# Feed-forward output of a two-layer decoder step: four of eight output tiles computed as two pairs of seven products for the last six inner tiles

## The chip, the cores and the metric

The kernel runs on one core of a Trainium2 chip. The metric is the device time of one execution, in microseconds. The engines are TensorE (PE, with its weight loads PEld), VectorE (DVE), ScalarE (ACT), GpSimd (POOL) and SyncE (SP), which here issues the loads from HBM.

## What is computed

One inference step of two layers for 512 prompt tokens and 64 sample tokens (576 columns, handled as two halves of 288). Each layer has a feed-forward block ahead of its mixer and one behind it, so there are four feed-forward passes. The change is in the output product of each pass, `(silu(a) * b) @ w_out`:

```
D_MODEL = 1024
D_FF = 2816
...
def half_swiglu(x, g, w_in, w_out):
    a, b = jnp.split(rms_norm(x, g) @ w_in, 2, axis=-1)
    return x + 0.5 * ((jax.nn.silu(a) * b) @ w_out)
...
for i in range(DEPTH):
    x = half_swiglu(x, norm_w[i, 0], w_ffn_in[i, 0], w_ffn_out[i, 0])
    x = x + mixer_i(rms_norm(x, norm_w[i, 1]))
    x = half_swiglu(x, norm_w[i, 2], w_ffn_in[i, 1], w_ffn_out[i, 1])
```

## The kernel before

**Numbers.** Every factor is split into a high part (`hw`, `hh`, `uah`) and a low part (`lw`, `hl`, `ual`); a product of 128 x 128 weights with 288 columns is made three times: high by high, high by low, low by high. Activations lie with features on partitions: D_MODEL is 8 tiles of 128 (`x[:, m, :]`), D_FF is 22 inner tiles (`TILES`).

**Units.** A pass is `NU = 30` units. Units 0 and 1 compute inner tiles in the plain way, the other inner tiles and most of the output by the scheme of Strassen in Winograd's form: blocks 1 to 7 ("products", `times(s, p)`) in place of eight. Four of the seven need differences of weight blocks (`diff1`, `diff2`, `diff34` on VectorE into `tw`, their high parts by `high12` and `high34` on ScalarE, their low parts by `low12` and `low34` on VectorE), three take the blocks as they come (`direct`: a copy and a negation on ScalarE, then an accumulating transfer issued by GpSimd, `add_direct`). On the other side they need sums and differences of halves of the hidden tiles (`h_side3`, `h_sides` on VectorE, places S1 to S4 of `hr`; high parts by `high_hs`, low parts by `low_hs`).

**Where the output is made.** Inner tiles 0 to 7 and 8 to 15 go into the output by the units 9 to 12 and 21 to 24 (`FAST_OUT`), each a pair of output tiles, 4 x 3 matrix products in each of the seven; VectorE adds each product to `x` (`add_product`), and the next product into the same bank waits for that (`x_part`). The last `KO = 6` inner tiles, 16 to 21, are multiplied plainly after the last unit: eight output tiles of 6 x 3 x 2 = 36 matrix products. `first_outs` interleaves tiles 0 and 1 with product 4 of the last unit; `out` does the others, which wait for `x_done`, the addition of the tile two before; the last tile of the last pass is made by halves. ScalarE makes the high part of each tile's weights (`high_out`, L1056), GpSimd the low part by a subtraction (L828), SyncE loads them (`out_unit`, L619). VectorE adds a whole tile to `x` (`add_out`, L2620) and right after that prepares tile m for what follows: the low part for the mixer (`low_u`, L2288) or, after the second pass, the sides of the next pass (`side` L2365, `side_sums` L2372 to L2378, `low_s` L2352), and adds squares for the norm (L2294).

**What sets the order.** Each engine's program is written out by hand, and semaphores with counts connect them: `prod_done` counts products of TensorE, `x_part` and `x_done` additions, `unit_done` output tiles. An instruction waits with everything behind it on its engine. Nothing is scheduled by a planner; `product_order` and `update_order` only number the products and additions.

**The last unit before the end**, `inner` of unit 29: VectorE does `gate_half` (L2399) of the tile before, its `hidden` (L2407), its low part (L2420), and then five operations of `sums` (L2428 to L2439), with `add_product` at L2476 in output units.

## Time and profile before

| what | us |
|---|---|
| median of 3 runs | 2453.65 (2452.84 to 2457.1) |
| profiled execution, whole | 2449.32 |
| its span in the trace | 2447.5 |
| first end: from the first output tile of the first pass to the mixer's first product | 350.04 to 390.1 |
| second end (followed at once by the third pass) | 1281.2 to 1321.3 |
| third end | 1656.8 to 1696.9 |
| fourth end, up to the tile by halves | 2393.8 to 2434.0 |

In the profile's views a line such as L2620 is a line of the kernel; "sb_" stands ahead of tiles in on-chip memory, "ps" is the accumulator memory of TensorE. Idle time is put down to the wait that ended last. The profiled execution is one run, and 4.3 us below the median of the others.

### The profile page before, as it was taken

The page shows a single profiled execution, that of the slowest core. Times are in us where ns is not written, and L with a number is a line of the kernel's source. Part 1 is how long each engine was busy: PE and PEld are TensorE (multiplying, and loading weights), DVE is VectorE, ACT ScalarE, POOL GpSimd, SP SyncE. Part 2 cuts the span into 40 slices and gives each one's busy share as a digit, 9 for nine tenths or more (in the row PEclk, how much of TensorE's full clock was granted, in tenths as well). Part 3 has the DMA queues.
Part 4 walks back from the last instruction along what each step waited for, and adds up shares of the span by engine and source line. Part 5 has one row for each costly group of instructions (what it writes and reads, how often), then busy time and mean ns, then how long its engine had stood idle before and what let it go on. Part 6 is the DMA issues. An engine that isn't in the chain of part 4 may idle for free.

```text
span 2447.5 us, 50261 instructions
## 1 busy us (share of the span) xinstructions
PE 2414.4 (99%) x19713; PEld 2362.0 (97%) x19713; DVE 1837.7 (75%) x3054; ACT 1392.9 (57%) x2388; POOL 755.4 (31%) x739
## 2 busy tenths in 40 slices
PE   8999999999999999999999999999999999999998
PEld 8999999999999989999999999999999998999998
DVE  8979766977777788978876988875235438988875
ACT  7757553545555556757666766664223227767663
POOL 1222224545555542222223222224322321222222
PEclk9999999999999999999999999999999999999999
DMA  6677753133333325676765677764433434677762
GB/s 192 162 170 166 171 118 111 49 103 106 106 106 97 106 83 147 152 177 160 175 139 137 150 172 162 172 148 134 158 131 122 136 110 111 158 172 162 174 149 88
DMA packets 105686, 339.01 MB, mean 139 GB/s; under 512 B 13776, under 2 KB 17360, under 8 KB 87184
## 3 DMA queue, kind: packets, MB, share of 16 engines
q1 hardware_dynamic: 53936, 242.40, 30.0%
q0 software_dynamic: 51552, 93.87, 22.8%
q8 instruction: 137, 2.24, 0.4%
q14 instruction: 61, 0.50, 0.1%
HBM read 223.06 MB, written 19.32 MB: 99 GB/s over the span
## 4 chain that ended last, share of the span: by engine, by line
PE 94%; DVE 4%; ACT 1%; issue 1%; DMA 0%; SPq 0%; POOL 0%; DVEq 0%; ACTq 0%
PE ps L1644 17%; PE ps L1642 17%; PE ps L1652 17%; PE ps L1540 7%; PE ps L1548 7%; PE ps L1541 7%; PE ps L1661 2%; PE ps L1662 2%; PE ps L1669 2%; PE ps L1591 1%; PE ps L1581 1%; PE ps L1582 1%; PE ps L1980 1%; PE ps L1982 1%; PE ps L1981 1%; DVE sb_acc L2713 1%
## 5 line engine op out<-in xcount | busy, mean ns | idle before, releaser
L1644 PE MATMUL ps<-sb_ual,sb_hw 128*128 128x288 f32 x2240 | 614.2, 296 | 0.0
L1642 PE MATMUL ps<-sb_uah,sb_hw 128*128 128x288 f32 x2240 | 610.7, 295 | 0.1
L813 POOL DMA_DIRECT2D sb_lw<-sb_rawf x328 | 282.3, 866 | 961.6 <-ACT sb_lw L987 944.8
L1642 PEld LDWEIGHTS ps<-sb_uah,sb_hw 128*128 128x128 f32 x2240 | 421.0, 188 | 0.7 <-issue 0.5
L1644 PEld LDWEIGHTS ps<-sb_ual,sb_hw 128*128 128x128 f32 x2240 | 421.2, 188 | 0.0
L796 POOL TENSOR_TENSOR sb_wl<-sb_raw,sb_wh 128x512 fp32r<-128x512 f32 (+1 forms) x170 | 282.4, 1678 | 389.8 <-ACT sb_wh L956 377.3
L1652 PE MATMUL ps<-sb_uah,sb_lw 128*128 128x288 f32 x2240 | 385.0, 294 | 0.0
L1540 PE MATMUL ps<-sb_uh,sb_wh 128*128 128x288 f32 x1360 | 373.6, 301 | 0.1
L1541 PE MATMUL ps<-sb_ul,sb_wh 128*128 128x288 f32 x1360 | 366.8, 296 | 0.0
L1652 PEld LDWEIGHTS ps<-sb_uah,sb_lw 128*128 128x128 f32 x2240 | 328.3, 188 | 0.7 <-DVE sb_lw L2336 0.4
L1540 PEld LDWEIGHTS ps<-sb_uh,sb_wh 128*128 128x128 f32 x1360 | 255.7, 188 | 7.6 <-issue 5.0
L985 ACT CAST sb_hw<-sb_rawf 128x512 fp32r<-128x512 f32 x336 | 207.7, 618 | 87.8 <-PE ps L1652 72.6
L1541 PEld LDWEIGHTS ps<-sb_ul,sb_wh 128*128 128x128 f32 x1360 | 255.8, 188 | 0.5
L1644 PE MATMUL ps<-sb_hl,sb_hw 128*128 128x288 f32 x896 | 243.9, 295 | 0.0
L1642 PE MATMUL ps<-sb_hh,sb_hw 128*128 128x288 f32 x896 | 243.2, 293 | 0.0
L956 ACT CAST sb_wh<-sb_raw 128x1024 fp32r<-128x1024 f32 (+1 forms) x106 | 111.5, 1052 | 199.6 <-PE ps L1548 127.5
L2341 DVE TENSOR_TENSOR sb_lw<-sb_tw,sb_hw 128x1024 fp32r<-128x1024 f32 x112 | 137.1, 1224 | 92.7 <-ACT sb_hw L1022 88.6
L987 ACT ACTIVATE sb_lw<-sb_rawf 128x512 fp32r<-128x512 f32 x328 | 206.5, 629 | 0.0
L1548 PE MATMUL ps<-sb_uh,sb_wl 128*128 128x288 f32 x1360 | 195.3, 296 | 0.2 <-POOL sb_wl L796 0.2
L1022 ACT CAST sb_hw<-sb_tw 128x1024 fp32r<-128x1024 f32 x112 | 117.7, 1051 | 124.2 <-PE ps L1652 124.2
L1548 PEld LDWEIGHTS ps<-sb_uh,sb_wl 128*128 128x128 f32 x1360 | 186.1, 190 | 0.9 <-POOL sb_wl L796 0.5
L1644 PEld LDWEIGHTS ps<-sb_hl,sb_hw 128*128 128x128 f32 x896 | 168.4, 188 | 0.0
(366 smaller groups left out, 5096.3 us busy)
## 6 DMA issues: line engine op xcount, KB each, us to landing
sb_lw<-sb_rawf POOLq DMA_DIRECT2D x358, 256.0 KB, 3.7
sb_rawf<-w_ffn_in SPq DMA_DIRECT2D x87, 1024.0 KB, 5.0
sb_rawf<-w_ffn_so SPq DMA_DIRECT2D x32, 1024.0 KB, 5.0
sb_raw<-w_ssd SPq DMA_DIRECT2D x64, 512.0 KB, 3.6
sb_raw<-w_att SPq DMA_DIRECT2D x40, 512.0 KB, 3.7
sb_rawf<-w_ffn_out SPq DMA_DIRECT2D x32, 384.0 KB, 3.1
sb_h<-state SPq DMA_DIRECT2D x8, 1024.0 KB, 5.1
ssm_sample<-sb_h SPq DMA_DIRECT2D x8, 1024.0 KB, 4.8
```

Of the source, the lines that this page charges most:

```text
L796: ins = pool.tensor_tensor(wl[parity][:, c], raw[:, parity, c], wh[parity][:, c].bitcast(F32), ALU.subtract)
L813: pool.dma_start(slot(lw, p), rawf[:, s % 2, i * BL:(i + 1) * BL], accum_op=ALU.add).then_inc(ld_in[i], 16)
L985: nc.scalar.copy(slot(hw, p), src).then_inc(hd_done, 1)
L987: nc.scalar.activation(slot(lw, p), src, ACT.Copy, scale=-1.0).then_inc(nd_done, 1)
L1022: nc.scalar.copy(slot(hw, 7, 2), tw[:, 2 * BL:4 * BL]).then_inc(ht34_done, 1)
L1540: pe.matmul(ps[:, b, 0:n], w, rh[:, k, t0:t0 + n], start=first and k == 0, stop=False)
L1541: pe.matmul(ps[:, b, 0:n], w, rl[:, k, t0:t0 + n], start=False, stop=False)
L1548: ins = pe.matmul(ps[:, b, 0:n], w, rh[:, k, t0:t0 + n], start=False, stop=last and k == nk - 1)
L1642: pe.matmul(out, w[:, k * P:(k + 1) * P], high[k], start=begins and k == 0, stop=False, skip_group_check=True)
L1644: pe.matmul(out, w[:, k * P:(k + 1) * P], low[k], start=False, stop=False, skip_group_check=True)
L1652: ins = pe.matmul(out, v[:, k * P:(k + 1) * P], high[k], start=False, stop=k == 3, skip_group_check=True)
L2341: V.tensor_tensor(slot(lw, 7, 2), tw[:, 2 * BL:4 * BL], slot(hw, 7, 2).bitcast(F32), ALU.subtract).then_inc(lt34_done, 1)
```

## The change

A pass has two more units, 30 and 31 (`NU = 32`, `E0`, `E1`). They make output tiles 2, 3 and 4, 5 from inner tiles 16 to 21 as seven products of 3 x 3 matrix products each. Output tiles 0, 1 and 6, 7 (`OUT_TILES`) stay plain, 36 matrix products each. So:

- The last six inner tiles form three pairs (`c == 2`); `h_side3`, `h_sides`, `high_hs` and `low_hs` now run for them too. Their fourth sum (A12 less S2) has a place of its own, `hr[:, 3, ...]`, with its own high part (`high_s4_out`) and low part (`low_s4_out`). Tiles 20 and 21 are kept in `he` and `ge`.
- SyncE loads tiles 0 and 1, then the two new units (`w_ffn_se`, 4 x 384 columns), then tiles 6 and 7. ScalarE and GpSimd get three `direct` blocks for each new unit, and four tiles instead of eight. The weight places of the new units are in another order (`END_SLOT`).
- On VectorE the last `gate_half` stands ahead of the first difference of weights of unit 30, as does the rest of the tile's end; then come the additions of the new units, mixed with the preparation of finished tiles (`next_sides`), in the order 0, 1, 3, 2, 5, 4, 6, 7 (`ORDER`), which the readers of the prepared tiles follow.
- On TensorE the units stand between `first_outs` and tile 6; product 4 of unit 31 stands within tile 6.

```diff
-NU = 30
+NU = 32
+OUT_TILES = (0, 1, 6, 7)
+END_SLOT = {1: 3, 5: 4, 6: 5, 2: 6, 3: 0, 7: 1, 4: 2}
...
                 first_outs(f)
-                for m in range(2, KD - 1 if f == 3 else KD):
-                    out(f, m)
+                s = f * NU + E0
+                for p in (1, 2, 5, 6, 3, 7):
+                    times(s, p)
+                times(s + 1, 1)
+                times(s + 1, 5)
+                times(s, 4)
+                times(s + 1, 6)
+                times(s + 1, 2)
+                times(s + 1, 3)
+                times(s + 1, 7)
+                u = U_FFN[f] + OUT_TILES.index(6)
+                free_out(f, 6)
+                pe.wait_ge(wh_done, u + 1)
+                out_highs(f, 6, range(2))
+                times(s + 1, 4)
+                out_highs(f, 6, range(2, KO))
+                pe.wait_ge(wl_done, u + 1)
+                out_lows(f, 6, range(KO)).then_inc(unit_done, 1)
+                if f < 3:
+                    out(f, 7)
...
                 gate_half(last)
+                diff1(e)
                 hidden(last)
+                diff2(e)
                 low_h(last)
+                diff34(e)
+                h_sides(f, 2, 2)
+                low12(e)
+                low_hs(f, 2, 2)
+                low_s4_out(f)
+                diff1(e1)
+                diff2(e1)
...
+                add_product(e, 1)
+                add_out(0)
+                add_out(1)
+                add_product(e, 2)
+                add_product(e, 5)
+                low34(e)
+                add_product(e, 6)
+                diff34(e1)
+                low12(e1)
+                add_product(e, 3)
+                add_product(e, 7)
+                next_sides(0)
+                add_product(e1, 1)
+                add_product(e1, 5)
+                next_sides(1)
+                add_product(e, 4)
+                add_product(e1, 6)
+                low34(e1)
+                add_product(e1, 2)
+                add_product(e1, 3)
+                add_product(e1, 7)
+                next_sides(3)
+                add_product(e1, 4)
+                next_sides(2)
+                next_sides(5)
+                next_sides(4)
+                add_out(6)
...
                 last = f * NU + LAST
+                direct(last + 1, 1)
                 silu(last)
                 high_h(last)
+                high12(last + 1)
+                direct(last + 1, 2)
+                high_hs(f, 2, 2)
+                direct(last + 1, 3)
+                high_s4_out(f)
+                high34(last + 1)
```

The first place is VectorE around the end of unit 29 in the first pass. Before, `sb_hr` and `sb_hl` are the tile of unit 28 (hidden and its low part), then come the five sums, the last gate, and the last tile:

```order
L2407 TENSOR_TENSOR sb_hr<-sb_hr,sb_gr 128x2x288
L2420 TENSOR_TENSOR sb_hl<-sb_hr,sb_hh 128x2x288
L2428 TENSOR_TENSOR sb_gr<-ps,sb_gr 128x288
L2431 TENSOR_TENSOR sb_hr<-ps,sb_hr 128x288
L2435 TENSOR_TENSOR sb_gr<-sb_gr,sb_rms 128x288
L2437 TENSOR_TENSOR sb_hr<-sb_hr,sb_pc 128x288
L2439 TENSOR_TENSOR sb_hr<-sb_hr,sb_rms 128x576
L2399 TENSOR_TENSOR sb_gr<-ps,sb_rms 128x288
L2407 TENSOR_TENSOR sb_hr<-sb_hr,sb_gr 128x576
L2420 TENSOR_TENSOR sb_hl<-sb_hr,sb_hh 128x576
L2620 SCALAR_TENSOR_TENSOR sb_x<-ps,sb_x 128x576
```

Now, at the same place (`sb_he` is tile 20):

```order
L2500 TENSOR_TENSOR sb_he<-sb_he,sb_gr 128x576
L2540 TENSOR_TENSOR sb_hr<-sb_he 128x288
L2514 TENSOR_TENSOR sb_hl<-sb_he,sb_hh 128x2x288
L2562 TENSOR_TENSOR sb_hl<-sb_hr,sb_hh 128x864
L2522 TENSOR_TENSOR sb_gr<-ps,sb_gr 128x288
L2525 TENSOR_TENSOR sb_ge<-ps,sb_ge 128x288
L2529 TENSOR_TENSOR sb_gr<-sb_gr,sb_rms 128x288
L2531 TENSOR_TENSOR sb_ge<-sb_ge,sb_pc 128x288
L2533 TENSOR_TENSOR sb_ge<-sb_ge,sb_rms 128x576
L2492 TENSOR_TENSOR sb_gr<-ps,sb_rms 128x288
```

Two operations (L2540, L2562) have come in between the hidden tile and the five sums. Between that last gate (L2492) and the first addition to x (L2585) now stand:

```order
L2410 TENSOR_TENSOR sb_tw<-sb_rawf 128x512
L2500 TENSOR_TENSOR sb_ge<-sb_ge,sb_gr 128x576
L2416 TENSOR_TENSOR sb_tw<-sb_rawf,sb_tw 128x512
L2514 TENSOR_TENSOR sb_hl<-sb_ge,sb_hh 128x576
L2423 TENSOR_TENSOR sb_tw<-sb_rawf,sb_tw 128x1024
L2549 TENSOR_TENSOR sb_hr<-sb_ge,sb_he 128x288
L2550 TENSOR_TENSOR sb_hr<-sb_ge,sb_hr 128x288
L2552 TENSOR_TENSOR sb_hr<-sb_ge,sb_hr 128x288
L2429 TENSOR_TENSOR sb_lw<-sb_tw,sb_hw 128x1024
L2562 TENSOR_TENSOR sb_hl<-sb_hr,sb_hh 128x864
L2568 TENSOR_TENSOR sb_hl<-sb_hr,sb_hh 128x864
L2410 TENSOR_TENSOR sb_tw<-sb_rawf 128x512
```

(and one more L2416). Before, two of these twelve stood there. The second place is ScalarE at the same time. Before, after the copy of the last sum (L1032), `silu`, the high part of the tile and the weights of output tiles:

```order
L1032 COPY sb_hr<-ps 128x288
L1037 ACTIVATE sb_gr<-sb_gr 128x576
L1043 CAST sb_hh<-sb_hr 128x576
L1056 CAST sb_hw<-sb_rawf 128x768 x2
L967 ACTIVATE sb_uh<-sb_x,sb_gains 128x576
```

Now:

```order
L1070 COPY sb_ge<-ps 128x288
L1021 CAST sb_hw<-sb_rawf 128x512
L1023 ACTIVATE sb_lw<-sb_rawf 128x512
L1075 ACTIVATE sb_gr<-sb_gr 128x576
L1081 CAST sb_hh<-sb_ge 128x576
L1050 CAST sb_hw<-sb_tw 128x1024
L1021 CAST sb_hw<-sb_rawf 128x512
L1023 ACTIVATE sb_lw<-sb_rawf 128x512
L1086 CAST sb_hh<-sb_hr 128x864
L1021 CAST sb_hw<-sb_rawf 128x512
L1023 ACTIVATE sb_lw<-sb_rawf 128x512
L1090 CAST sb_hh<-sb_hr 128x864
```

The blocks of the new unit stand between the steps of the last tile, and the high part of the fourth sums (L1090) stands behind two of them. The third place is VectorE in the second end, ahead of the additions of output tiles 6 and 7 (L2740). Before, the addition of tile 6 (L2620) stood behind the preparation of tile 5:

```order
L2620 SCALAR_TENSOR_TENSOR sb_x<-ps,sb_x 128x576
L2365 SCALAR_TENSOR_TENSOR sb_ual<-sb_x,sb_gains,sb_uah 128x2x288
L2372 SCALAR_TENSOR_TENSOR sb_us<-sb_x,sb_gains,sb_us 128x288
L2375 TENSOR_TENSOR sb_us<-sb_us 128x288
L2377 TENSOR_TENSOR sb_us<-sb_us 128x288
L2378 SCALAR_TENSOR_TENSOR sb_s<-sb_x,sb_gains,sb_us 128x288
L2294 TENSOR_TENSOR sb_ssq<-sb_ssq,sb_sqx 128x576
L2352 TENSOR_TENSOR sb_ual<-sb_us,sb_uah 128x3x288
L2620 SCALAR_TENSOR_TENSOR sb_x<-ps,sb_x 128x576 x2
```

Now the preparation of tiles 5 and 4 stands in one piece behind the last product's addition and that of tile 2:

```order
L2458 SCALAR_TENSOR_TENSOR sb_ual<-sb_x,sb_gains,sb_uah 128x2x288
L2383 TENSOR_TENSOR sb_ssq<-sb_ssq,sb_sqx 128x576
L2458 SCALAR_TENSOR_TENSOR sb_ual<-sb_x,sb_gains,sb_uah 128x2x288
L2465 SCALAR_TENSOR_TENSOR sb_us<-sb_x,sb_gains,sb_us 128x288
L2468 TENSOR_TENSOR sb_us<-sb_us 128x288
L2470 TENSOR_TENSOR sb_us<-sb_us 128x288
L2471 SCALAR_TENSOR_TENSOR sb_s<-sb_x,sb_gains,sb_us 128x288
L2383 TENSOR_TENSOR sb_ssq<-sb_ssq,sb_sqx 128x576
L2445 TENSOR_TENSOR sb_ual<-sb_us,sb_uah 128x3x288
L2740 SCALAR_TENSOR_TENSOR sb_x<-ps,sb_x 128x576 x2
```

The same group of L2458 to L2445 stands twice more ahead of it, for tiles 0 and 1 and for tiles 3 and 2.

## Rows read from the trace of the kernel before

**Rows 1.** The page: busy time by engine, and the last chain by engine.
```profile
PE 2414.4 (99%) x19713; PEld 2362.0 (97%) x19713; DVE 1837.7 (75%) x3054; ACT 1392.9 (57%) x2388; POOL 755.4 (31%) x739
...
PE 94%; DVE 4%; ACT 1%; issue 1%; DMA 0%; SPq 0%; POOL 0%; DVEq 0%; ACTq 0%
```

**Rows 2.** Windows over first and second end: length, busy by engine, clock, DMA.
```profile
350.04:390.10 40.06, 40.00 (x303) 39.77 (x302) 23.46 (x28) 16.36 (x24) 14.13 (x8) 1.00 0.27 83
1281.20:1321.30 40.10, 40.04 (x302) 39.65 (x301) 27.73 (x41) 21.61 (x35) 13.80 (x8) 1.00 0.35 112
```

**Rows 3.** Chain in order of time, first end: start us, us, what.
```profile
364.96 1.57 PE ps L1669 x12
...
369.72 1.57 PE ps L1669 x12
```

**Rows 4.** Line L2620 (output tile added to x): who waited for it, us, times.
```profile
  PEld ps L1661: 1.3, 5
```

**Rows 5.** VectorE's timeline, first end: start us, us, instruction, idle before it.
```profile
347.99 1.73 DVE L2420 TENSOR_TENSOR sb_hl<-sb_hr,sb_hh 128x576 fp32r<-128x576 f32 x1 [0.74 <-ACT sb_hh L1043]
349.64 0.45 DVE L2428 TENSOR_TENSOR sb_gr<-ps,sb_gr 128x288 f32<-128x288 f32 x1
...
350.37 1.37 DVE L2435 TENSOR_TENSOR sb_gr<-sb_gr,sb_rms 128x288 f32<-128x288 f32 x1
...
352.14 0.76 DVE L2439 TENSOR_TENSOR sb_hr<-sb_hr,sb_rms 128x576 f32<-128x576 f32 x1
353.06 0.46 DVE L2399 TENSOR_TENSOR sb_gr<-ps,sb_rms 128x288 f32<-128x288 f32 x1 [0.16 <-PE ps L1652]
354.27 0.76 DVE L2407 TENSOR_TENSOR sb_hr<-sb_hr,sb_gr 128x576 f32<-128x576 f32 x1 [0.75 <-ACT sb_gr L1037]
355.77 0.76 DVE L2420 TENSOR_TENSOR sb_hl<-sb_hr,sb_hh 128x576 fp32r<-128x576 f32 x1 [0.74 <-ACT sb_hh L1043]
```

**Rows 6.** GpSimd's timeline, first end.
```profile
347.26 4.16 POOL L828 TENSOR_TENSOR sb_lw<-sb_rawf,sb_hw 128x768 fp32r<-128x768 f32 x2 [6.50 <-ACT sb_hw L1056]
```

**Rows 7.** Groups of VectorE, whole span: busy us, mean ns, idle before.
```profile
L2341 DVE TENSOR_TENSOR sb_lw<-sb_tw,sb_hw 128x1024 fp32r<-128x1024 f32 x112 | 137.1, 1224 | 92.7 <-ACT sb_hw L1022 88.6
...
L2476 DVE SCALAR_TENSOR_TENSOR sb_x<-ps,sb_x 128x288 f32<-128x288 f32 x224 | 98.1, 453 | 23.2 <-PE ps L1652 22.9
...
L2317 DVE TENSOR_TENSOR sb_tw<-sb_rawf 128x512 f32<-128x512 f32 x112 | 76.6, 684 | 9.4 <-DMA sb_rawf<-w_ffn_in 7.6 <-DMA sb_rawf<-w_ffn_so 1.9
...
L2620 DVE SCALAR_TENSOR_TENSOR sb_x<-ps,sb_x 128x576 f32<-128x576 f32 x31 | 23.4, 754 | 33.1 <-PE ps L1669 33.1
```

**Rows 8.** Groups of ScalarE, whole span.
```profile
L985 ACT CAST sb_hw<-sb_rawf 128x512 fp32r<-128x512 f32 x336 | 207.7, 618 | 87.8 <-PE ps L1652 72.6 <-PE ps L1591 9.8 <-DMA sb_rawf<-w_ffn_so 5.5
...
L1083 ACT CAST sb_uah<-sb_us 128x864 fp32r<-128x864 f32 x16 | 14.3, 909 | 5.2 <-DVE sb_s L2378 5.2
```

**Rows 9.** VectorE's timeline, second end.
```profile
1296.83 0.82 DVE L2365 SCALAR_TENSOR_TENSOR sb_ual<-sb_x,sb_gains,sb_uah 128x576 fp32r<-128x576 f32 x1 [0.84 <-ACT sb_uah L1066]
1297.69 0.52 DVE L2372 SCALAR_TENSOR_TENSOR sb_us<-sb_x,sb_gains,sb_us 128x288 f32<-128x288 f32 x1
1298.24 0.46 DVE L2375 TENSOR_TENSOR sb_us<-sb_us 128x288 f32<-128x288 f32 x1
...
1299.54 0.75 DVE L2294 TENSOR_TENSOR sb_ssq<-sb_ssq,sb_sqx 128x576 f32<-128x576 f32 x1
1300.60 1.06 DVE L2352 TENSOR_TENSOR sb_ual<-sb_us,sb_uah 128x864 fp32r<-128x864 f32 x1 [0.31 <-ACT sb_uah L1083]
```

**Rows 10.** The page, DMA issues: count, KB each, us to landing.
```profile
sb_lw<-sb_rawf POOLq DMA_DIRECT2D x358, 256.0 KB, 3.7
sb_rawf<-w_ffn_in SPq DMA_DIRECT2D x87, 1024.0 KB, 5.0
...
sb_rawf<-w_ffn_out SPq DMA_DIRECT2D x32, 384.0 KB, 3.1
```

**Rows 11.** Waits, all engines: engine line, waited for, us in total, times, longest.
```profile
DVE sb_gr L2399 <- PE ps L1652: 62.5, 56, 2.8
```

More of the change, by code:

```diff
@@ L110, in update_order @@
     for f in range(4):
-        for i in OPENING:
+        for i in OPENING[0:2]:
             u = f * NU + i
@@ L116, in update_order @@
             yield from ((u + 3, 7), (u + 3, 4))
+        u = f * NU + E0
+        yield from ((u, p) for p in (1, 2, 5, 6, 3, 7))
+        yield from ((u + 1, 1), (u + 1, 5), (u, 4), (u + 1, 6), (u + 1, 2), (u + 1, 3), (u + 1, 7), (u + 1, 4))
 DONE = {key: i + 1 for i, key in enumerate(product_order())}
@@ L627, in ffn @@
             def ffn(f):
-                for n in range(NU):
+                for n in range(E0):
                     if n < 2 and f:
@@ L640, in ffn @@
                         store_samples(GROUPS - 1)
-                for m in range(KD):
+                for m in OUT_TILES[0:2]:
+                    out_unit(f, m)
+                for n in (E0, E1):
+                    blocks(f * NU + n)
+                for m in OUT_TILES[2:]:
                     out_unit(f, m)
@@ L812, in add_direct @@
                 pool.wait_ge(nd_done, nth_negative(s, p))
-                pool.dma_start(slot(lw, p), rawf[:, s % 2, i * BL:(i + 1) * BL], accum_op=ALU.add).then_inc(ld_in[i], 16)
+                pool.dma_start(slot(lw, s, p), rawf[:, s % 2, i * BL:(i + 1) * BL], accum_op=ALU.add).then_inc(ld_in[i], 16)
             def ffn(f):
-                for n in range(NU):
+                for n in range(E0):
                     s = f * NU + n
@@ L1012, in high12 @@
                 else:
[L1013 to L1014 removed]
+                    act.wait_ge(prod_done, DONE[s - 1, 7 if s % NU == E0 else 6])
+                nc.scalar.copy(slot(hw, s, 5, 2), tw[:, 0:2 * BL]).then_inc(ht12_done, 1)
             def high34(s):
@@ L1210, in ffn @@
                 full_units(f)
-                for n in range(FULL, NU):
+                for n in range(FULL, E0):
                     s = f * NU + n
@@ L1532, in product @@
                 pe.wait_ge(wh_done, u + 1)
-                for k in range(nk):
+                order = range(nk) if chunk is None else [m - ORDER[chunk % KD] // 4 * 4 for m in ORDER[chunk % KD:chunk % KD + nk]]
+                for i, k in enumerate(order):
                     if between and k == at:
@@ L1565, in full @@
                 if n == 0 and part == 0 and f == 2:
-                    pe.wait_ge(x_done, KD * f - 1 + 2)
+                    pe.wait_ge(*tile_done(1, 6))
                 if part == 1 and n == 1:
                     pe.wait_ge(sqrt_ready, NORM_OF_FFN[f] + 1)
-                for m in range(KD):
+                for i, m in enumerate(ORDER if f == 2 and n == 0 and part == 0 else range(KD)):
                     if part == 0 and n == 1 and m == KD // 2:
@@ L1629, in times @@
                     pe.wait_ge(s_ready, 5 * f + 5)
-                if opening and p in (1, 2):
+                if n == E0 and p == 3:
+                    pe.wait_ge(hs_ready, nth_split(f, 2, 3) + 1)
+                if opening and p in (1, 2) and n < E0:
                     pe.wait_ge(h_ready, TILES * f + 8 * c + (7 if p == 1 else 8))
                 if n in FAST_OUT:
-                    high, low = ([h[:, k, SIDE[p], :] for k in range(4)] for h in (hh, hl))
+                    high, low = ([h[:, 3, at + k, :] if n >= E0 and p == 3 else h[:, k, SIDE[p], :] for k in range(pairs)]
+                                 for h, at in ((hh, 4), (hl, 0)))
                 else:
                     high, low = ([a[:, SIDE[p], k, :] for k in range(4)] for a in (uah, ual))
-                w, v, out = slot(hw, p), slot(lw, p), ps[:, bank, 0:HALF]
-                for k in range(4):
+                w, v, out = slot(hw, s, p), slot(lw, s, p), ps[:, bank, 0:HALF]
+                for k in range(pairs):
                     if n == FULL and p == 5:
@@ L1739, in ffn @@
             def ffn(f):
-                for n in range(NU):
+                for n in range(E0):
                     s = f * NU + n
@@ L2574, in inner @@
                         h_sides(f, c, j)
+                        if c == 2 and j == 1:
+                            low_h(s - 2)
                         low_h(s - 1)
@@ L2605, in ffn @@
                 full_units(f)
-                for n in range(FULL, NU):
+                for n in range(FULL, E0):
                     s = f * NU + n
@@ L3241, in laid_out @@
     w_out = []
+    w_end = []
     for i in range(2):
```

275 lines of the change are left out of this document (170 added, 105 removed).

## The prediction

> **What bounds the kernel now.** The chain that ended last comes first: 94% of the span is TensorE work [rows 1]. The windows over the ends of the four feed-forward passes, which hold all of the change, come next: TensorE is busy 40.00 of 40.06 us in the first end and 40.04 of 40.10 in the second, at granted clock 1.00, and the other two read alike [rows 2]. So matrix products that go away are worth their full time, and any wait of TensorE is paid in full. VectorE is the next to look at: 23.5 us of the first end, but 27.7 of the second, where it also makes the factors of the following pass, and GpSimd is far from full [rows 1, 2]. An output tile is 36 products, and the last twelve of two successive tiles start 4.76 us apart [rows 3], so one product costs 0.132 us.
>
> **What goes away.** Before, an end has 8 tiles x 36 = 288 products; after, 4 x 36 + 2 units x 7 x 9 = 270. That is 18 fewer, 2.38 us per end, 9.5 us in four. The wait of TensorE before output tile 2 (1.3 us over 5 places [rows 4], 0.26 apiece) goes too: I take 0.24 per end. If nothing else moved, the gain would be 4 x 2.62 = 10.5 us.
>
> **What is added on VectorE, and where TensorE meets it.** After the first product of a unit, TensorE may only go on when VectorE has read the bank: product 6 waits for the addition of product 1, product 3 for that of 5, product 7 for that of 6. In the code order VectorE does, before the addition of the first product: the end of the last gate, two differences, the large difference, three sums, two low parts of sums, the low part of the weights, and two differences of the second unit. I follow this on the clock of the first end.
>
> Step 1, the start of that queue. Before, VectorE waited for TensorE and began the last gate scaling (L2399) at 353.06 [rows 5]. After, two more operations stand in the unit ahead (a tile's difference and a pair's low part, 0.45 and about 1.05 us: the 864-wide row of the second end says 1.06 [rows 9]). They meet the two GpSimd subtractions that occupy 347.26 to 351.42 [rows 6]. Rows show what such a meeting costs: L2420 took 1.73 us against 0.76 at 355.77, L2435 1.37, while L2428, which reads PSUM, took its 0.45 between them [rows 5]. Each blocked operation ended about 0.62 (576 wide) or 0.32 us (288) after the subtraction did. So: the new difference is ready at 347.28, is held to 349.10 and ends at 349.4; the low part is held by the second subtraction, which itself is held to 349.4 and ends about 351.2, so it ends 351.8; the pair's low part ends 352.8. Then come the five sums; they took 349.64 to 352.81 less the 0.92 that L2435 lost, 2.25 us. The gate scaling starts at 355.0, 2.0 us later than before. In the trace of before the same blocking cost nothing, since VectorE then waited for TensorE.
>
> The Trainium skill, "SBUF — State Buffer", section "SBUF: two separate sides", calls the ports that VectorE and GpSimd share an exclusive lock, held for a whole instruction, against VectorE operations with two SBUF inputs. The trace agrees (1.73 against 0.76 us). Were the blocking absent for the added operations, the gate would start at 353.06 still, which is a case below.
>
> Step 2, from there to the first addition: gate to hidden 1.21, hidden to low part 1.50 (353.06, 354.27, 355.77: ScalarE's part lies inside, and so does one difference) [rows 5]; the low part 0.76; the large difference, as wide as the low weights, 1.22; three sums of 288 columns at 0.45; low weights 1.22; low sums 1.05 [rows 7, 9]. Then a wait of 0.8 for ScalarE, which has a copy of 0.62 and a negation, taken at the same, in front of its 0.91 copy of the fourth sums [rows 8]; low fourth sums 1.05; two differences 0.68; the addition 0.45 [rows 7]. Together 12.0; successive operations overlap by 0.08, some nine times, so 11.4. The first bank is free at 355.0 + 11.5 = 366.5.
> TensorE reaches that place earlier: the two first output tiles end at 361.3 as before, three products of nine take 3.56, and the low block of product 2 arrives about 0.35 late (copy, negation, then 3.7 us to landing [rows 10]). That is 365.2, so it waits 1.3 to 1.4.
>
> Step 3. In front of the addition of product 5 stand two output tiles (0.75 each) and an addition: 2.1 us after product 6 could start, against 1.19 of work, so 0.95 more. In front of the addition of product 6 stand the low weights, 1.22 + 0.45: 0.34 more. The waits of an end come to 0.35 + 1.4 + 0.95 + 0.34 = 3.05. Against 2.62 that is a loss of 0.43 per end, 1.7 us in four.
>
> Step 4, the second end. After the addition of product 6 TensorE has 8 products of nine, two output tiles and a last product of nine: 153 x 0.132 = 20.2 us, and then needs the bank of tile 6, which VectorE must have added. VectorE has in front of that, in program order: large difference and low weights 1.22 x 3; ten additions 0.45; six side parts 0.82; three groups of four side sums (0.52, 0.46, 0.46 and again about 0.51) 1.95; five additions of squares 0.75; three low parts 1.06; the tile itself 0.75 [rows 7, 9]. That is 26.6 us in 40 operations; 40 overlaps of 0.08 take off 3.3; waits within side sums (six of 0.12) and for ScalarE (three of 0.31 [rows 9]) add 1.6; the two GpSimd subtractions of tiles 6 and 7 now fall on it and add 2.2 by the price of step 1. So 27.1 to 27.5, and TensorE idles 7.0 to 7.3 us, partly inside the second unit and partly ahead of the next pass. Before, this work lay in 40 us with 12 to spare.
>
> **What costs nothing.** The differences of tiles 2 to 5 of the last six lie in units where VectorE waits for TensorE, up to 2.8 us at the last gate [rows 11]. GpSimd does four subtractions fewer and six accumulations more per end, at 31% busy [rows 1]. The load for the first unit (768 KB, between 3.1 us for 384 KB and 5.0 for 1024 [rows 10], so 4.3) starts when the first subtraction ends, 349.1, and is there at 353.4, when the gate has not started; 1 us more would be covered, 3 us more would not. The reordering of the last tiles changes nothing by itself.
>
> **Sum.** 4 x 0.43 + 7.2 = 8.9, say 9 us slower. Against the profiled execution (2449.3 with the 1.8 us around its span) that is 2458.3; the median of the runs shown is 4.3 higher, and I put the change on that: 2453.65 + 9 = 2462.7.
>
> **Rivals.**
> A. VectorE's extra queue is not held by GpSimd. The gate starts at 353.06, and the first wait is 0.9 in place of 1.75: an end is then 0.4 better than before, and step 4 costs 5.1 (27.5 less 2.2, against 20.2). Sum 5.1 - 1.6 = +3.5: 2457.2. For it: the operations could slip into the gap between the two subtractions, as they start within 0.1 us of one another. Against: two rows with the full price.
> B. Faster: the additions keep up. It would need the first addition within the 3.6 us of three products, and in the second end a queue of at most 20.2 us; then the gain is the 10.5 less about 1.4 of small waits: 2444.5. The decision point is VectorE's queue of 26.6 us of work; it would have to be a quarter shorter than its rows. I see nothing that makes it so.
> C. The loads of the new weights land late. They queue behind the output tiles and beside the accumulations of GpSimd. From 1 us over 4.3 on each us goes on the chain four times: 2 us late gives +13.7, 2467.4. Against: transfers of 1024 KB took 5.0 in the median.
> D. The change does not take the time out that it says, because products of nine pay something at each change of bank. 14 changes per end; a bound from the windows is 0.06 idle in 40 us with as many changes, so at most 0.2 per end: inside the range.
>
> **Chances.** Forecast 0.66, A 0.16, B 0.04, C 0.10; 0.04 is left for mixtures in which half of step 4 is hidden, at +1 to +4. The range 2457 to 2468 takes in A and C. A measurement of this kernel can tell 0.2%, 4.9 us. Slower than that: forecast and C nearly whole and a little of A, 0.79; within: 0.15; faster: 0.06.
>
> **What would show it.** In the profile after: the windows of the ends show TensorE idle about 3 us in the first, third and fourth and about 10 in the second; the waits list gives the products of the units waiting for the additions to x; TensorE waits some 3.5 us ahead of the third pass; VectorE's low parts at 347 to 352 last 1.4 to 2.4 us; VectorE is gapless through the second end. Wrong would be: first addition before 365 (step 1 or 2), the third pass starting less than 3 us later relative to the second (step 4), or a wait on a load.

## The result, and the profile after

The changed kernel takes 2460.8 us (median of 9 runs, 2458.67 to 2465.32) against 2452.91 of the kernel before (9 runs): ratio 1.0036, 95% interval 1.0025 to 1.0046, so 8.8 us slower by the ratio (the two medians alone differ by 7.9). Differences between kernels are given by their ratios from here on. Run again beside three other kernels it took 2460.19 against 2451.84, ratio 1.0037 (1.0024 to 1.0050). Forecast were 2462.7 and 9 us slower.

The page of after, its rows on busy time and on the last chain, to be laid beside [rows 1]:

```profile
PE 2411.8 (98%) x19641; PEld 2356.1 (96%) x19641; DVE 1914.5 (78%) x3198; ACT 1435.2 (58%) x2452; POOL 746.2 (30%) x747
...
PE 83%; DVE 10%; ACT 3%; issue 3%; DMA 1%; SPq 0%; POOL 0%; DVEq 0%; ACTq 0%
```

TensorE has 72 products fewer (18 in each of four ends) but VectorE's share of the last chain went from 4 to 10%: TensorE now waits for it. The windows over the first three ends, from the first output tile to the first product of the next stage, have the columns of [rows 2], with the bounds set to a hundredth. The two rows behind them are pieces of the first end:

```profile
347.94:389.38 41.44, 39.43 (x284) 38.89 (x283) 37.26 (x55) 25.25 (x38) 12.15 (x10) 0.96 0.46 112
1281.30:1328.57 47.27, 39.09 (x285) 37.62 (x283) 44.97 (x69) 30.07 (x48) 12.11 (x10) 1.00 0.48 129
1666.54:1706.86 40.32, 38.25 (x285) 37.47 (x283) 36.96 (x54) 25.68 (x38) 13.19 (x10) 1.00 0.50 124
366.70:369.80 3.10, 3.10 (x14) 3.10 (x15) 3.10 (x4) 1.12 (x3) 0.00 (x0) 0.50 0.98 219
369.80:372.90 3.10, 3.10 (x25) 3.10 (x25) 2.39 (x5) 2.89 (x5) 0.86 (x1) 1.00 0.35 61
```

Before, by the same count, these ends took 39.97, 40.16 and 39.97 us. The third is the clean case: 0.35 longer, with TensorE idle for 2.1 us of it (the waits are 3.1 us by their weight loads, since each starts while the last product still counts as busy). The second is 7.1 longer, with VectorE busy for 45.0 of 47.3 us. The first is 1.5 longer, and its two pieces say why it isn't 0.35: for 3.1 us TensorE's granted clock was 0.50, its lower level of 1.2 GHz, with 14 products where the next 3.1 us hold 25. No part of the forecast had that.

The waits list of after (engine, line, waited for; us in total, times, longest) names whom TensorE waits for:

```profile
PE ps L1708 <- DVE sb_x L2585: 6.8, 5, 1.4
PE ps L1636 <- DVE sb_x L2740: 4.9, 1, 4.9
...
PE ps L1708 <- issue: 2.3, 4, 0.6
...
PE ps L1718 <- DMA sb_lw<-sb_rawf: 0.7, 2, 0.4
```

L1708 is a product of nine, L2585 the addition of a product to x, L2740 the addition of an output tile, L1636 the third pass's first products. The 1.3 us before output tile 2 [rows 4] are gone. In the timeline of TensorE in the first end the two waits are:

```profile
364.51 0.37 PE L1708 MATMUL ps<-sb_hh,sb_hw 128*128 128x288 f32 x1 [1.43 <-DVE sb_x L2585]
...
366.52 0.58 PE L1708 MATMUL ps<-sb_hh,sb_hw 128*128 128x288 f32 x1 [0.58 <-issue]
```

The profile puts the second down to "issue". It is the wait for the addition of product 5: the experiments below move it by moving work ahead of that addition. Counted from one weight load to the next, beyond the pace of 0.132, these waits are 1.69 and 0.85 us; I give waits in this way from here on.

VectorE in the first end, beside [rows 5], and GpSimd, beside [rows 6]:

```profile
345.31 2.16 DVE L2540 TENSOR_TENSOR sb_hr<-sb_he 128x288 f32<-128x288 f32 x1
347.40 2.39 DVE L2514 TENSOR_TENSOR sb_hl<-sb_he,sb_hh 128x576 fp32r<-128x576 f32 x1
349.71 1.05 DVE L2562 TENSOR_TENSOR sb_hl<-sb_hr,sb_hh 128x864 fp32r<-128x864 f32 x1
...
352.94 0.45 DVE L2492 TENSOR_TENSOR sb_gr<-ps,sb_rms 128x288 f32<-128x288 f32 x1
...
361.61 1.06 DVE L2568 TENSOR_TENSOR sb_hl<-sb_hr,sb_hh 128x864 fp32r<-128x864 f32 x1 [0.74 <-ACT sb_hh L1090]
...
363.91 0.45 DVE L2585 SCALAR_TENSOR_TENSOR sb_x<-ps,sb_x 128x288 f32<-128x288 f32 x1
```

```profile
345.30 3.87 POOL L862 TENSOR_TENSOR sb_lw<-sb_rawf,sb_hw 128x768 fp32r<-128x768 f32 x2 [6.09 <-ACT sb_hw L1097]
```

This execution reached its first output tile at 347.94, 2.1 us sooner than the trace of before (350.04), so 2.1 is to be added to compare clocks. The last gate scaling (L2492) then stands at 355.0, and it has no wait for TensorE any more: before it began at 353.06 with VectorE idle ahead of it [rows 5].

### The profile page after: what moved, and what is told of

Same layout as the page of the kernel before. It is cut to its first block, busy times and chain, and to the rows that moved or that the text cites. A ratio compares the mean times of both kernels' runs of the same rounds, so it can differ in the third digit from the quotient of the medians.

```text
span 2461.4 us, 50493 instructions
## 1 busy us (share of the span) xinstructions
PE 2411.8 (98%) x19641; PEld 2356.1 (96%) x19641; DVE 1914.5 (78%) x3198; ACT 1435.2 (58%) x2452; POOL 746.2 (30%) x747
## 4 chain that ended last, share of the span: by engine, by line
PE 83%; DVE 10%; ACT 3%; issue 3%; DMA 1%; SPq 0%; POOL 0%; DVEq 0%; ACTq 0%
PE ps L1710 17%; PE ps L1708 16%; PE ps L1718 16%; PE ps L1595 7%; PE ps L1603 7%; PE ps L1596 6%; PE ps L2068 1%; PE ps L2070 1%; PE ps L2069 1%; PE ps L1636 1%; PE ps L1637 1%; PE ps L1646 1%; DVE sb_acc L2865 1%; PE ps L2253 1%; PE ps L1925 1%
## 5 line engine op out<-in xcount | busy, mean ns | idle before, releaser
L843 POOL DMA_DIRECT2D sb_lw<-sb_rawf x352 | 302.9, 863 | 1029.6 <-ACT sb_lw L1023 1012.1
L1708 PE MATMUL ps<-sb_uah,sb_hw 128*128 128x288 f32 x2240 | 611.1, 295 | 0.5 <-ACT sb_hr L1070 0.5
L1708 PEld LDWEIGHTS ps<-sb_uah,sb_hw 128*128 128x128 f32 x2240 | 420.2, 188 | 1.3 <-issue 1.0
L1708 PE MATMUL ps<-sb_hh,sb_hw 128*128 128x288 f32 x1064 | 292.1, 296 | 9.3 <-DVE sb_x L2585 6.8
L1710 PE MATMUL ps<-sb_hl,sb_hw 128*128 128x288 f32 x1064 | 291.9, 297 | 0.0
L1021 ACT CAST sb_hw<-sb_rawf 128x512 fp32r<-128x512 f32 x360 | 222.5, 618 | 105.8 <-PE ps L1718 78.0
L1023 ACT ACTIVATE sb_lw<-sb_rawf 128x512 fp32r<-128x512 f32 x352 | 221.6, 629 | 0.0
L2434 DVE TENSOR_TENSOR sb_lw<-sb_tw,sb_hw 128x1024 fp32r<-128x1024 f32 x120 | 146.8, 1223 | 92.8 <-ACT sb_hw L1060 88.5
L1708 PEld LDWEIGHTS ps<-sb_hh,sb_hw 128*128 128x128 f32 x1064 | 201.0, 189 | 11.7 <-issue 10.1
L1710 PEld LDWEIGHTS ps<-sb_hl,sb_hw 128*128 128x128 f32 x1064 | 201.4, 189 | 0.0
L1060 ACT CAST sb_hw<-sb_tw 128x1024 fp32r<-128x1024 f32 x120 | 126.2, 1052 | 127.0 <-PE ps L1718 127.0
```

What stands on the lines that cost most here:

```text
L843: pool.dma_start(slot(lw, s, p), rawf[:, s % 2, i * BL:(i + 1) * BL], accum_op=ALU.add).then_inc(ld_in[i], 16)
L1021: nc.scalar.copy(slot(hw, s, p), src).then_inc(hd_done, 1)
L1023: nc.scalar.activation(slot(lw, s, p), src, ACT.Copy, scale=-1.0).then_inc(nd_done, 1)
L1060: nc.scalar.copy(slot(hw, s, 7, 2), tw[:, 2 * BL:4 * BL]).then_inc(ht34_done, 1)
L1708: pe.matmul(out, w[:, k * P:(k + 1) * P], high[k], start=begins and k == 0, stop=False, skip_group_check=True)
L1710: pe.matmul(out, w[:, k * P:(k + 1) * P], low[k], start=False, stop=False, skip_group_check=True)
```

## The experiments

Each was compared with the kernel before on the same chip. "Against after" is the difference of two such comparisons, with 8.8 us for after; one of them is uncertain by about 2 us either way. The lengths of ends come from each kernel's own trace.

**The second end: side sums put off.** The additions for the third pass's sums leave the second end and are made in the third pass.

```
                     if f == 1:
                         side(2, m)
-                        if i % 2:
-                            side_sums(2, m // 2)
...
-                    if f == 1 and i % 2:
-                        low_s(2, m // 2)
...
                 else:
+                    side_sums(f, 0)
+                    side_sums(f, 1)
+                    for i in range(4):
+                        low_s(f, i)
+                        if i < 2:
+                            side_sums(f, i + 2)
                     dve.wait_ge(s_ready, 5 * f + 4)
```

ScalarE's operations for these sums move in the same way.

> Changed against the kernel after: in the second end the four groups of side sums and their low parts (VectorE's three or four sums and one 864-wide low part per pair of tiles, ScalarE's copies for them) no longer stand between the side parts of the tiles but behind all of them, in the third pass. Nothing is left out. My theory (step 4, VectorE's queue is what TensorE waits for at the end of the second pass): each group holds VectorE about 3.0 us, four of them 12, so that of the 27.2 us between the addition of product 6 and that of tile 6 some 15 to 16 stay, against 20.2 of TensorE. TensorE's waits of 1.47, 0.30 and 5.19 us in the trace after go, 7.0 in all, and up to 0.8 of it may come back where the third pass first uses the sums: 6 to 7 us faster than the kernel after, 2 to 3 slower than before (2454.5 to 2455.5). Rival (the third pass starts late for another reason, such as the weights or the side parts of its first tiles): the 5.19 stays, and at most 2 us are gained.

Measured: 2453.35 against 2452.09, ratio 1.0007 (0.9997 to 1.0016), that is 7 us faster than after. The window over the second end:

```profile
1281.05:1321.39 40.34, 38.26 (x285) 37.49 (x284) 35.70 (x53) 26.70 (x41) 12.51 (x11) 1.00 0.59 155
```

It is as long as the third end. Of TensorE's 7.0 us of later waits nothing is left there, and waits of 0.94 and 0.79 us came up in the third pass, 1.7 where up to 0.8 was expected. So the late third pass was VectorE's queue. This trace has no stretch at the lower clock in any end, though all four still hold the waits of 1.6 and 0.85 us.

**GpSimd's subtractions for output tiles 0 and 1, cut to 8 of 768 columns.**

```
+                    n = 8 if o < 2 else KO * P
-                    w = slice(out_place(m), out_place(m) + KO * P)
+                    w = slice(out_place(m), out_place(m) + n)
```

> Left out against the kernel after: the GpSimd subtractions for output tiles 0 and 1 work on 8 of their 768 columns, so the low parts of these weights are stale. My theory (step 1): the two VectorE operations that lasted 2.16 and 2.39 us at 345.3 and 347.4 in the trace after last 0.45 and 0.76, the last gate scaling starts about 2.0 us earlier, and the first unit's weights are there before it; TensorE's wait for the addition of product 1 falls from 1.7 to 0.3 to 0.7, and its 0.2 for the low block goes: 1.1 to 1.35 us in each of four ends, 4.4 to 5.4 in all (the second end too, since its queue starts earlier). Case A of the prediction (no such blocking on the path): 0 us, within 0.5.

Measured: 2455.76, ratio 1.0018 (1.0009 to 1.0027), 4.4 us faster than after. VectorE's timeline (its lines are one higher than in after):

```profile
345.71 0.50 DVE L2541 TENSOR_TENSOR sb_hr<-sb_he 128x288 f32<-128x288 f32 x1
346.42 0.76 DVE L2515 TENSOR_TENSOR sb_hl<-sb_he,sb_hh 128x576 fp32r<-128x576 f32 x1 [0.21 <-ACT sb_hh L1082]
...
351.35 0.46 DVE L2493 TENSOR_TENSOR sb_gr<-ps,sb_rms 128x288 f32<-128x288 f32 x1 [0.95 <-PE ps L1719]
```

The two operations have their own times, 0.50 and 0.76 in place of 2.16 and 2.39, and the gate starts 3.0 us behind the first output tile (348.33), as in before (353.06 less 350.04), in place of 5.0 as in after. It waits for TensorE again. TensorE's first wait fell from 1.65 to 0.82, a little less than expected, and the 0.2 us for the low block went: the third end is 39.3 long in place of 40.3. The 5.2 us ahead of the third pass stay, with 6.8 us at the lower clock around their end (from 1323.4). The blocking exists and is on the path, so case A is out.

**The same for output tiles 6 and 7** (`o > 1` in place of `o < 2`).

> Left out against the kernel after: the GpSimd subtractions for output tiles 6 and 7 work on 8 of their 768 columns. My theory: in the second end they took 2.0 us from VectorE's full queue (2.40 for a 0.75 addition of squares and 1.20 for a 0.82 side part), and TensorE waited for the end of that queue: 2.0 us faster than after, nearly all in the second end. Rival (the second end's queue has slack at this place, the late third pass being ScalarE's or a load's doing): within 0.5 us of after.

Measured: 2457.78, ratio 1.0024 (1.0015 to 1.0032), 2.9 us faster than after. In the trace the second end is 45.72 us long, 1.5 less than in after, all of it in the wait ahead of the third pass (5.2 to 3.7), and the third is unchanged (40.3). So taking the subtractions away is worth 1.5 us there, not the 2.0 that I expected: VectorE then waited 0.40 us for TensorE once. The first end of this trace has after's waits of 1.6 and 0.85 us but no stretch at the lower clock, and is 40.1 long in place of 41.4. Nothing in the edit reaches these waits, so that isn't its work; what the median has beyond 1.5 isn't placed.

**Only the two differences of the second unit, behind the first addition.**

```
                 low_s4_out(f)
-                diff1(e1)
-                diff2(e1)
...
                 add_product(e, 1)
+                diff1(e1)
+                diff2(e1)
                 add_out(0)
```

> Changed against the kernel after: VectorE makes the two differences of the second unit's weights (0.68 us each) behind the addition of product 1 in place of ahead of it. Nothing is left out. Theory Q (VectorE's queue up to the addition of product 5 is the limit, whatever stands ahead of which addition): the wait of TensorE for the first addition falls by about 1.4 us, that for the addition of product 5 rises by the same, and the time is that of the kernel after within 1 us. Theory F (the first bank's release is the price, as the 1.7 us wait by itself reads): 1.4 us gained per end, 5.5 us in four.

Measured: 2463.02, ratio 1.0046 (1.0031 to 1.0061). In its trace the wait for the first addition is 0.30 (from 1.69) and that for the addition of product 5 is 2.18 (from 0.85); with the low block's they come to 2.71, where after has 2.72 (0.18 for the low block), and the span is 2461.4, the same as after's. Theory Q holds in the trace and F falls: a wait that is read off one place doesn't say what its removal is worth. The median came out 2 us over after's, outside the 1 us of Q but no more than the comparison is uncertain by, and the granted clock, averaged over its runs, is 0.990 against 0.992. Its trace has 3.4 us at the lower clock behind the 2.18 us waits in three of four ends, and 6.8 us from within the long wait ahead of the third pass.

**The kernel after, once more.**

> The kernel after once more, unchanged, beside the two that follow and with a trace of its own. What is open: the profile of after lasts 13.9 us longer than that of before while the medians differ by 8.8, and it has three stretches of about 3.3 us, right behind waits of TensorE (366.7, 1328.9, 2424.6 us), in which a product takes 0.24 in place of 0.132 us, 4.4 us lost in all. Theory K (the clock falls behind long waits, and it is part of the price): again two to four such stretches, each behind a wait of 1.5 us or more, and 7 to 11 us over before. Theory R (they are chance, as in any kernel): stretches elsewhere or none.

Measured: 2460.19, ratio 1.0037 (1.0024 to 1.0050). Two stretches at the lower clock stand in its ends, at the places of the first trace:

```profile
347.64:389.03 41.39, 39.43 (x285) 38.83 (x283) 37.25 (x55) 25.23 (x38) 12.19 (x10) 0.96 0.46 111
...
366.40:369.40 3.00, 3.00 (x13) 3.00 (x14) 3.00 (x4) 1.01 (x3) 0.00 (x0) 0.50 1.03 232
1328.50:1332.00 3.50, 3.50 (x15) 3.50 (x16) 2.71 (x4) 3.50 (x8) 1.25 (x3) 0.51 0.80 136
```

The first follows waits of 1.63 and 0.85 us, the second one of 5.2 us. Products that take 0.24 in place of 0.132 us cost 1.4 and 1.5 us. The third of the first trace, in the fourth end, isn't there. By its count theory K is met, but not for both places. The traces of x_defer and x_sub67 hold the first end's two waits at the same length, and their clock stays at 1.00. The pair stands in 20 ends of five traces (after, x_after2, x_defer, x_sub67, x_load), and the clock fell behind it in four of them. The wait ahead of the third pass, 3.7 to 5.2 us, stands in seven traces (after, x_after2, x_sub01, x_sub67, x_diffs, x_order, x_load), and the clock fell at it in all seven. So the stretch there belongs to this kernel; the one in the first end comes in some executions. Over all runs, the mean granted clock is 0.992 for after, both times, against 0.994 for before.

**VectorE's order alone.** All in the last two units; the low fourth sums go behind the first addition, the additions of products 5 and 6 ahead of what only later products need.

```
-                low_s4_out(f)
...
                 add_product(e, 1)
-                add_out(0)
-                add_out(1)
+                low_s4_out(f)
                 add_product(e, 2)
                 add_product(e, 5)
-                low34(e)
+                add_out(0)
                 add_product(e, 6)
-                diff34(e1)
+                low34(e)
+                add_out(1)
                 low12(e1)
                 add_product(e, 3)
                 add_product(e, 7)
+                diff34(e1)
                 next_sides(0)
```

> Changed against the kernel after: VectorE's order in the last two units alone. The low part of the fourth sums stands behind the addition of product 1; the additions of products 2, 5 and of tile 0 follow, then the low weights and the additions of product 6 and tile 1; the second unit's low weights and the additions of products 3 and 7 come ahead of its large difference and of the next norm's work. Nothing is left out. Theory Q (the queue in front of each addition is the price): TensorE's waits of an end fall from 3.05 us to about 1.75 in ends 1, 3 and 4, and in the second end the later waits take back what the first give, since VectorE has no gap there; 4 to 5 us faster than after by the waits, and up to 4 more if the stretches at the lower clock go with the waits of 1.5 us and more: 2452 to 2457. Rival (order within the queue doesn't matter, its length does): within 1 us of after.

Measured: 2455.66, ratio 1.0013 (1.0005 to 1.0022), 5.6 us faster than after. The first and third end are 39.1 us long (after: 41.4 with its slow stretch, and 40.3). In the second end, where VectorE has no gap, the 5.2 us ahead of the third pass stay and a wait of 2.1 us comes up for the low block of the second unit's first product. Behind that wait the clock is at its lower level for 3.4 us, and from within the wait ahead of the third pass for 6.8, so this end is 48.4 long, 1.1 more than in after. Order alone pays in three ends and not in the one whose queue is too long.

**Both together.** The order of x_order and the put-off sums of x_defer, with nothing left out.

> Both at once: the order of x_order, and the side sums of the third pass made inside the third pass as in x_defer. Nothing is left out. If the additions' queue in each end (3.05 us of waits) and the second end's queue (7.0) are the two causes of the loss, then 1.3 us go four times and 6 to 7 once: 11 to 12.5 us faster than after, and with the stretches at the lower clock up to 4 more, so 2445 to 2449.5, which is 0.1 to 0.3% under before. Were something else of the change at work (products of nine that cost more, case D, or loads), it stays at or above before.

Measured: 2448.72 against 2451.84, ratio 0.9987 (0.9978 to 0.9996): 3.2 us faster than before, 12.0 faster than after. The same three ends:

```profile
349.62:388.71 39.09, 38.33 (x284) 37.49 (x283) 35.91 (x54) 24.88 (x38) 12.30 (x10) 1.00 0.48 115
1278.62:1317.79 39.17, 38.70 (x285) 37.57 (x283) 36.06 (x53) 26.60 (x41) 12.23 (x11) 1.00 0.62 162
1654.98:1694.10 39.12, 38.40 (x285) 37.48 (x284) 36.72 (x54) 25.57 (x38) 13.32 (x10) 1.00 0.52 128
```

Each is 0.9 to 1.0 us shorter than before, the clock is 1.00 in all, and the mean clock of its runs is that of before (0.994).

**And all four subtractions cut to 8 columns.**

> x_all, and left out: all four GpSimd subtractions of output tiles in every end work on 8 of 768 columns (stale low parts). Then VectorE is held up nowhere in the ends, and the waits of an end fall to at most 0.4 us. Expected: 4 to 5 us faster than x_all, 8 to 10 under before, which is the 10.5 us of my term for the products and waits that went away, less what is left of waits. If case D is true (products of nine pay at each change of bank) it is at most 6 under before.

Measured: 2445.02, ratio 0.9972 (0.9961 to 0.9983), 6.9 us under before; expected were 8 to 10. The ends:

```profile
347.68:385.85 38.17, 37.84 (x285) 37.41 (x284) 33.05 (x53) 25.36 (x38) 8.12 (x9) 1.00 0.47 115
1277.53:1315.71 38.18, 37.90 (x285) 37.46 (x283) 31.97 (x51) 26.81 (x41) 7.33 (x10) 1.00 0.61 160
```

They are 1.8 and 2.0 us shorter than before, the third (38.28) 1.7. The waits that are left come to 0.9 us (0.31 ahead of a product, 0.56 for the low block of the second unit's first product) where I expected 0.4 at most, and 0.94 and 0.67 us come up in the third pass. With the waits counted, the term of 18 products at 0.132 us stands: TensorE is busy 37.84 in such an end, against 39.91 less 2.38, or 37.53, by a second trace of before. By the weight loads it is closer: 38.17 less its waits of 0.87 is 37.30, and 39.97 less 0.35 (the wait before output tile 2) is 39.62, a difference of 2.32 against 2.38. Case D can have 0.1 to 0.3 us per end, not more. The interval of the ratio alone, 4 to 10 us, wouldn't decide it.

**The kernel before, once more.**

> The kernel before once more, unchanged, for a second trace of it. What is open: its one trace lasts 3.6 us less than its median, and has no stretch at the lower clock in the four feed-forward ends. If the stretches in the ends of after belong to its waits, this one has none there either, its ends again last 39.97, 40.16 and 39.97 us from the first output tile to the next stage's first product, and what differs from the first trace lies outside of the ends. If they are chance, one or two may show here.

Measured: 2451.87, ratio 1.0000 (0.9992 to 1.0009). Its ends:

```profile
348.25:388.22 39.97, 39.91 (x303) 39.68 (x302) 23.62 (x28) 16.35 (x24) 14.28 (x8) 1.00 0.27 82
1278.34:1318.52 40.18, 40.12 (x302) 39.74 (x301) 27.76 (x41) 21.72 (x35) 13.94 (x8) 1.00 0.34 112
1656.34:1696.32 39.98, 39.92 (x303) 39.69 (x302) 24.37 (x28) 16.68 (x24) 15.25 (x8) 1.00 0.28 86
```

The ends repeat to 0.02 us and show no slow stretch. What lies between them doesn't repeat like that: the first output tile stood at 350.04 and 348.25 in the two traces, and the third pass, counted between the second and the third end, lasted 335.4 and 337.8. So a few us per execution belong to neither kernel.

**The first unit's load two us later.**

```
                 if n >= E0:
-                    sp.wait_ge(wl_done, U_FFN[f] + n - E0 + 1)
+                    sp.wait_ge(wl_done, U_FFN[f] + 2)
```

> Changed against the kernel after: the load of the first unit's weights (768 KB) waits for the second subtraction of GpSimd too, and so starts about 2.0 us later. Nothing is left out. Case C of the prediction, by its own bounds (1 us of cover): 1 us per end, 4 us slower than after. Theory S (in the trace after, ScalarE's copy of these weights waits for the load until 351.83, and the last gate's ScalarE operation stands behind that copy and its negation; it began at 353.42): the copy starts at 353.8, the gate's operation at 354.9, and everything behind it is 1.5 us later: 5 to 6 us slower. Theory N (loads are covered): within 1 us.

Measured: 2470.8, ratio 1.0078 (1.0065 to 1.0091), 10 us slower than after. ScalarE's timeline in after, and in this run:

```profile
351.83 0.62 ACT L1021 CAST sb_hw<-sb_rawf 128x512 fp32r<-128x512 f32 x1 [3.17 <-DMA sb_rawf<-w_ffn_se]
...
353.42 0.69 ACT L1075 ACTIVATE sb_gr<-sb_gr 128x576 f32<-128x576 f32 x1 [0.44 <-DVE sb_gr L2492]
```

```profile
355.92 0.62 ACT L1021 CAST sb_hw<-sb_rawf 128x512 fp32r<-128x512 f32 x1 [5.04 <-DMA sb_rawf<-w_ffn_se]
356.45 0.63 ACT L1023 ACTIVATE sb_lw<-sb_rawf 128x512 fp32r<-128x512 f32 x1
356.98 0.67 ACT L1075 ACTIVATE sb_gr<-sb_gr 128x576 f32<-128x576 f32 x1
```

Against after, with the 2.2 us by which this execution was later all along, the copy stands 1.9 us later, the last gate's operation (L1075) behind it 1.3 later, and the third end is 1.45 us longer (41.78). In after that operation had waited 0.44 us for the gate, and 1.9 less 0.44 is 1.46. The four ends together are 6.5 longer, the fourth taken against the one of after without a slow stretch. That is S in kind and C too low, though the 10 us are well over the 5 to 6 of S. Some 3 us of the 10 are in none of the ends. What comes behind the fourth end lasts 1.3 us longer, with the clock low in 13.5 us of it in place of 9.3 to 9.5; the rest stays open.

**One exchange more on ScalarE in the third pass.**

```
-                if f == 2:
-                    side_in(f, 3)
                 high_full(s + 1, 2)
+                if f == 2:
+                    side_in(f, 3)
                 high_s(f, 2)
```

> x_all with one more exchange on ScalarE in the third pass: the third part of the second full unit's weights is copied and negated ahead of ScalarE's two 288-column products for the last pair's side sums. Nothing is left out. If the 0.94 us that TensorE waited in the third pass of x_all (at 1337.7) come from that place in ScalarE's queue, they go: 0.5 to 1 us faster than x_all, 3.5 to 4.5 us under before (0.15 to 0.18%).

Measured: 2449.39 against 2452.39, ratio 0.9988 (0.9979 to 0.9996), the same as x_all. The 0.94 us in the third pass shrank to 0.16, but the expected 0.5 to 1 us doesn't show in the median. The trace, of a run of 2454.4, shows a wait that can take their place. TensorE's and GpSimd's timelines in the second end:

```profile
1302.78 0.76 PE L1718 MATMUL ps<-sb_hh,sb_lw 128*128 128x288 f32 x3 [1.81 <-DMA sb_lw<-sb_rawf]
```

```profile
1296.58 0.86 POOL L843 DMA_DIRECT2D sb_lw<-sb_rawf  x1 [1.94 <-ACT sb_lw L1023]
```

An accumulation of 256 KB issued at 1296.58 landed at about 1302.7, 6.1 us later, where their median is 3.7. The same happened in the third end (6.2), and once in x_order. Each time 3.4 us at the lower clock followed. In x_all the same transfer, beside the same two others, took 3.6 and 4.9 us in these ends, so what makes it late isn't shown. With the queues shortened it is what comes last.

## Why the prediction was right

**Terms that held.** Each end without a slow stretch, by the two traces of each kernel: 40.33 after, 39.97 before, so +0.36; the forecast had +0.43. The waits in it are 0.2 for the low block, 1.65, 0.85 and 0.38, together 3.1; the forecast had 0.35, 1.4, 0.95 and 0.34, together 3.05. The wait that goes away, before output tile 2, was taken at 0.24; by the weight loads it is 0.35 in both traces of before, and that is most of the 0.07 between the two figures.

**Step 1**: the gate 2.0 us later, from one operation held by each subtraction. In the trace 2.16 and 2.39 us on two operations, and the gate 2.0 later by the first output tile. The subtractions cut (x_sub01) gave exactly these 2.0 back. The pair's low part behind them went through at its own 1.05, as forecast, and ended at 350.76, on the clock of before 352.9 (forecast 352.8).

The Trainium skill, "SBUF — State Buffer", section "SBUF: two separate sides", lets one of the two engines hold the shared ports for a whole instruction. The trace agrees: 2.39 and 0.76 us for the same operation with and without the subtraction.

**Step 2**: first addition done at 366.5. Measured 364.36, on the clock of before 366.5. The 11.4 us of chained operations were right to 0.1 (the forecast's own rows give 11.3, 12.0 less nine overlaps of 0.08, and its last line adds 11.5). **Step 3**: as above.

**Step 4**: the second end. Behind the addition of product 6 the forecast gave VectorE 27.1 to 27.5 us against 20.2 of TensorE; it took 27.2 (1301.3 to 1328.5). TensorE's waits were 1.48, 0.31 and 5.2, or 7.0, forecast 7.0 to 7.3; the end as a whole is 7.0 us longer than before (forecast 7.6). The split was off: I had named 3.5 us ahead of the third pass. The chain of waits there, in order of time, ends as forecast:

```profile
1325.85 0.92 ACT sb_uah L1126
...
1327.77 0.76 DVE sb_x L2740
...
1328.57 0.40 PE ps L1636
```

The second pair of subtractions was forecast at 2.2; the two operations that it held lost 2.0 in the trace (2.40 for 0.75 and 1.20 for 0.81), and without them the end is 1.5 shorter (x_sub67). x_defer then took 6.9 us out of this end by moving the sums alone, which is the direct proof of the step.

**What the forecast left out.** It priced a wait at its own length. Behind the longer ones the clock fell, 1.4 us in the first end and 1.5 at the start of the third pass in both traces of after, and 1.5 more in the fourth end of one. The ends alone (3 x 0.36, 7.0, and 0.4 more in the fourth, which is 0.77 longer) make 8.5, and with the clock 11 to 13, as the spans of the two traces of each kernel differ (11.3 on average). The comparison gives 8.8. Outside of the ends the traces show nothing that the change gives back: 2286 and 2287 us in before, 2289 and 2287 in after. The two traces of before lie 3.6 and 1.2 us under its median, those of after 2.5 over and 1.0 under its own, so the spans overstate; but 2 to 4 us between what the ends show with the clock and what the comparison shows aren't placed. So the mechanism is right, and that the sum of 9 met 8.8 so closely is in part luck: it left out a cost of 3 to 4 us, and the comparison came out lower than the traces by about as much.

**The rivals.** A fell with x_sub01. B names the right lever: the additions must keep up. x_all comes nearer to it by moving work alone, with nothing left out (3.2 us under before), and x_all_sub at 6.9 under with the subtractions cut; it isn't met because the queue as written is 27 us long. C was right in direction and too low: the load had landed at 351.83, only 1.1 us before the gate, and ScalarE's copy for it stands in front of the gate's own operation, which I hadn't followed. The 1 us of cover that I gave it wasn't there: 1.9 us more cost 1.45 per end. Its sum for 2 us, +13.7, doesn't follow from its own terms either: 8.9 and four times 1 is 12.9. D is bounded at 0.3 us.

## What to carry to other kernels

Work removed from the engine that bounds the kernel is worth its time only as long as that engine doesn't come to wait for another one's queue. Add up the other engine's queue between two hand-overs, and compare it with the bounding engine's work between the same two. A wait at one place is no price: shift what stands before it and see where the wait goes. An operation with slack (sums for a later stage) that stands in a full queue ahead of one without any is the first to be moved.

## What the runs showed of the hardware

TensorE's clock can fall behind waits that are 2.5 us together. After 1.69 and 0.85 us of waiting, with one product of nine between them, the granted clock was 0.50 for 3.1 us (366.70 to 369.80), and back at 1.00 for the next 3.1; the loss, 1.4 us, is over half of the two waits. Over the traces, the clock fell behind this pair of waits in 4 of 20 ends, behind a single wait of 2.1 to 2.2 us (x_diffs, x_order, x_best) in 6 of 7, and at a wait of 3.7 to 5.2 us in 7 of 7. With waits of 0.9 us and less in an end (x_all, x_all_sub) it stayed at 1.00 in all. What decides it for the pair, the runs don't show.

An accumulating transfer of 256 KB took 3.7 to 3.8 us in the median, and between 3.6 and 6.2 when it ran with another one and with a load of 384 KB.

In all eight ends of after's two traces each of GpSimd's subtractions for output tiles 0 and 1, alone 1.85 us long, held exactly one VectorE operation: one of 0.50 took 2.14 to 2.16 us, one of 0.76 took 2.38 to 2.40. The other way round it holds too. In the second end the subtractions for tiles 6 and 7 began at 1311.02, 0.02 us behind a VectorE operation of 1.21 us (L2434):

```profile
1311.02 5.23 POOL L862 TENSOR_TENSOR sb_lw<-sb_rawf,sb_hw 128x768 fp32r<-128x768 f32 x2 [7.36 <-ACT sb_hw L1097]
```

The two took 5.23 us in place of 3.87, and the first of them 2.91 in place of 1.86.
